# A six-stage fp32 network: two MLP norms and the third layer divide by the norm behind their products

## The reference

```python
def rmsnorm(x, g):
    xf = x.astype(jnp.float32)
    y = xf * lax.rsqrt(jnp.mean(xf * xf, axis=-1, keepdims=True) + EPS)
    return (y * g.astype(jnp.float32)).astype(x.dtype)

# stick_breaking_attention, for a block of 128 queries
z = jnp.einsum('bhqd,bhkd->bhqk', q_blk, kt).astype(jnp.float32) * scale
mask = kpos[None, :] < qpos[:, None]
log_keep = jnp.where(mask, jax.nn.log_sigmoid(-z), 0.0)
log_survive = lax.cumsum(log_keep, axis=3, reverse=True) - log_keep
weights = jnp.where(mask, jnp.exp(jax.nn.log_sigmoid(z) + log_survive), 0.0)

# the odd layer, and the MLP behind each layer
hn = rmsnorm(x, odd_norm[i])
q, k, v = jnp.split(hn @ odd_w_in[i], 3, axis=-1)
x = x + stick_breaking_attention(q, k, v) @ odd_w_out[i]
hn = rmsnorm(x, ffn_norm[layer])
x = x + (jax.nn.silu(hn @ ffn_w_gate[layer]) * (hn @ ffn_w_up[layer])) @ ffn_w_down[layer]
```

## Time and profile before

| | |
|---|---|
| runs | 1703.34, 1696.55, 1700.85 us, median 1700.85 |
| profiled execution | 1705.26 us, its span 1703.5 us |
| PE busy | 1597.6 us (94%) |
| DVE, ACT, POOL busy | 62%, 49%, 23% of the span |
| first MLP from norm to norm | 142.36 to 337.40 us |
| odd layer | 337.40 to 484.08 us |
| second MLP | 484.08 to 679.40 us |

### The profile page before, as it was taken

How to read it: one execution, slowest core, us unless ns; L and a number is a source line. 1 busy time by engine, 2 the same in 40 slices (tenths; PEclk the granted TensorE clock), 3 DMA queues, 4 the chain that set the end, 5 groups by cost and what they waited for, 6 DMA issues and landing times.

```text
span 1703.5 us, 32938 instructions
## 1 busy us (share of the span) xinstructions
PE 1597.6 (94%) x11807; PEld 1448.6 (85%) x11807; DVE 1053.7 (62%) x1973; ACT 832.7 (49%) x1228; POOL 393.4 (23%) x176
## 2 busy tenths in 40 slices
PE   7779999999799999896899989999999999999999
PEld 6668999898589999895689989999999777778887
DVE  7775555512235555717469993067887899985555
ACT  6456444458644444543355655544444444445453
POOL 2001000156330001562267898810000000000000
PEclk9879999999999999898899999999999999999999
DMA  5114555543255555342144545555545445555554
GB/s 215 63 57 134 184 186 186 179 137 100 75 199 185 185 185 181 124 131 72 62 149 164 177 154 166 184 167 164 169 160 166 156 168 167 169 163 195 195 188 159
DMA packets 72557, 264.88 MB, mean 155 GB/s; under 512 B 8080, under 2 KB 8336, under 8 KB 72112
## 3 DMA queue, kind: packets, MB, share of 16 engines
q1 hardware_dynamic: 71744, 261.20, 46.7%
q10 hardware_dynamic: 752, 2.83, 0.5%
HBM read 262.95 MB, written 1.05 MB: 155 GB/s over the span
## 4 chain that ended last, share of the span: by engine, by line
PE 82%; DVE 5%; POOL 5%; issue 4%; ACT 4%; DMA 0%; POOLq 0%; DVEq 0%; ACTq 0%
PE ps L495 25%; PE ps L497 24%; PE ps L496 24%; POOL w_lo L2109 5%; DVE arena L1441 2%; PE ps L972 2%; PE ps L552 1%; PE ps L808 1%; ACT xn L1074 0%; PE ps L588 0%; PE ps L652 0%; DVE w_lo L1441 0%; DVE x_s L1441 0%; ACT w_hi L1047 0%; ACT arena L1191 0%
## 5 line engine op out<-in xcount | busy, mean ns | idle before, releaser
L1047 ACT ACTIVATE w_hi<-ring 128x1024 fp32r<-128x1024 f32 x489 | 516.6, 1057 | 380.1 <-PE ps L497 371.4
L495 PE MATMUL ps<-hT_hi,w_hi 128*128 128x256 f32 x2216 | 639.5, 289 | 18.9 <-POOL w_lo L2109 11.5
L496 PE MATMUL ps<-hT_hi,w_lo 128*128 128x256 f32 x2216 | 628.9, 284 | 0.0
L497 PE MATMUL ps<-hT_lo,w_hi 128*128 128x256 f32 x2216 | 628.8, 284 | 0.0
L2109 POOL TENSOR_TENSOR w_lo<-ring,w_hi 128x1024 fp32r<-128x1024 f32 x151 | 378.8, 2519 | 679.4 <-ACT w_hi L1047 679.0
L1441 DVE TENSOR_TENSOR w_lo<-ring,w_hi 128x1024 fp32r<-128x1024 f32 x338 | 412.6, 1222 | 178.9 <-ACT w_hi L1047 178.5
L495 PEld LDWEIGHTS ps<-hT_hi,w_hi 128*128 128x128 f32 x2216 | 426.9, 193 | 26.1 <-ACT arena L1386 8.7
L496 PEld LDWEIGHTS ps<-hT_hi,w_lo 128*128 128x128 f32 x2216 | 427.2, 193 | 1.6
L497 PEld LDWEIGHTS ps<-hT_lo,w_hi 128*128 128x128 f32 x2216 | 426.7, 193 | 0.0
L495 PE MATMUL ps<-w_hi,a_hi 128*128 128x512 f32 x688 | 275.5, 400 | 3.4 <-DVE a_lo L1441 3.4
L497 PE MATMUL ps<-w_lo,a_hi 128*128 128x512 f32 x688 | 269.4, 392 | 0.0
(11 more groups left out here) (237 smaller groups left out, 1351.1 us busy)
## 6 DMA issues: line engine op xcount, KB each, us to landing
ring<-in_strips SPq DMA_DIRECT2D x489, 512.0 KB, 3.5
const<-in_const SPq DMA_DIRECT2D x1, 1544.0 KB, 12.2
x_s<-in_x SPq DMA_DIRECT2D x2, 512.0 KB, 4.6
arena<-in_rel ACTq DMA_DIRECT2D x1, 1024.0 KB, 6.0
arena<-in_keys ACTq DMA_DIRECT2D x1, 1024.0 KB, 6.4
out<-x_s SPq DMA_DIRECT2D x4, 256.0 KB, 2.1
arena<-in_ssm_bc SPq DMA_DIRECT2D x1, 512.0 KB, 6.8
arena<-in_ssm_b SPq DMA_DIRECT2D x1, 512.0 KB, 8.0
```

The costliest lines, as they stand in the source:

```text
L495: pe.matmul(out, l_hi, r_hi, start=start, stop=False, **kw)
L496: pe.matmul(out, l_lo, r_hi, start=False, stop=False, **kw)
L497: return pe.matmul(out, l_hi, r_lo, start=False, stop=stop, **kw)
L1047: sc.activation(w_hi[:, n % RING, :], ring[:, n % RING, :], ACT.Copy).then_inc(high_ready, 1)
```

## The change

1. In the three norms x is turned raw, by a PE transpose that waits for the residual sums (`raw_norm`). ACT's copies (`parts`) come between its two squares, DVE's ahead of the reciprocals. The diagonal of scales is spread to a row over all partitions by two fp32 products with ones (`widen_scale`) behind the first strips, and DVE copies it out (`take_scale`).
2. In the MLPs DVE multiplies the gate product by the row ahead of ACT's silu, and the up product in `combine`.
3. In the odd layer DVE scales q and k out of PSUM (`project`), ACT scales v per token. The softplus is masked on DVE (a product with 0 and 1) and split in two fp32r halves, and `cum` is two fp32r products for one in fp32. PE runs `z(j)` ahead of `cum(j-1)`; ACT runs `softplus(j)` ahead of `weights(j-1)`; the copies of `ov` move to DVE.
4. The end of the odd layer is written anew: the last pair's scores use banks 4 and 5, so that out strips 0 and 1 run ahead of its sums, and DVE makes the low halves of the out strips, not POOL.

```diff
+            def raw_norm(i):
+                for a in range(NT):
+                    for c in range(KC):
+                        if c % 4 == 0:
+                            pe.wait_ge(x_ready, 4 * (i - 1) + 2 * a + c // 4 + 1)
+                        at = (c % 2) * T + a * P
+                        mm = pe.transpose(ps[:, norm_bank(i, c // 2), at:at + P], x_s[:, a, c * P:(c + 1) * P],
+                                          ident)
+                        if a == NT - 1 and c % 2:
+                            mm.then_inc(turned, 1)
+            def widen_scale(i):
+                pe.wait_ge(diag_ready, NT * (i + 1))
+                for a in range(NT):
+                    mm = pe.matmul(ps[:, 0, a * P:(a + 1) * P], ones, scale_diag[:, a, :], start=True, stop=True)
+                mm.then_inc(scale_wide, 1)
...
                 gate_up(base, 4, fresh=STAGE_OF[name])
+                widen_scale(STAGE_OF[name])
...
-                    pe.wait_ge(sp_masked, j + 1)
+                    pe.wait_ge(sp_low, j + 1)
                     for h in (2 * j, 2 * j + 1):
-                        pe.matmul(ps[:, h % 4, 0:3 * P], k("neg_tri"), o_sp[:, h % 4, :], start=False,
-                                  stop=False, skip_group_check=True)
+                        b = z_bank(h)
+                        for part in (o_sp_hi, o_sp_lo):
+                            pe.matmul(ps[:, b, 0:3 * P], o_tri[:, :], part[:, h % 2, :], start=False, stop=False,
+                                      skip_group_check=True)
...
-                pe.wait_ge(w_masked, 8)
+                pe.wait_ge(w_masked, 7)
                 out_rows(1, "odd", range(2))
+                ov(6)
+                cum(7)
+                out_rows(1, "odd", range(2, 4))
                 ov(7)
-                out_rows(1, "odd", range(2, KC))
+                out_rows(1, "odd", range(4, KC))
...
+                def gate(strip, c, i=None):
+                    ve.wait_ge(strip_done, strip + 1 if i is None else UNROLL * i + (strip + 1))
+                    tt(f_silu[:, c % 2, :], ps[:, 4 + c % 2, 0:T], scale_row, ALU.mult).then_inc(gate_scaled, 1)
...
+                    tt(f_act[:, c % 2, :], ps[:, 6 + c % 2, 0:T], scale_row, ALU.mult).then_inc(up_scaled, 1)
...
+                take_scale(STAGE_OF[name])
+                gate(base, 0)
                 combine(base + 1, 0)
                 low(base + 3)
                 with ve.Fori(0, (FC - 2) // 2) as i:
                     for u in range(2):
                         at = base + 2 + 3 * u
+                        gate(at, 1 + u, i)
                         low(at + 2, i)
                         low(at + 3, i)
                         combine(at + 1, 1 + u, i)
                         low(at + 4, i)
...
+                    ve.wait_ge(sp_ready, j + 1)
+                    ch.link(tt(diagonal(sp), diagonal(sp),
+                               diagonal(bc(o_before, 1, [P, 2, 3 * P])), ALU.mult))
+                    ve.tensor_copy(o_sp_hi, sp).then_inc(sp_high, 1)
+                    ve.wait_ge(sp_high, j + 1)
+                    tt(o_sp_lo, sp, o_sp_hi.bitcast(F32),
+                       ALU.subtract).then_inc(sp_low, 1)
...
             po.wait_ge(low_ready, AT[("odd", "v", 0)])
             lows(("odd", "v", 0), ("odd", "v", 7))
...
+            lows(("odd", "q", 0), ("odd", "k", 1))
+            po.wait_ge(sp_low, 1)
+            lows(("odd", "q", 2), ("odd", "k", 7))
+            po.wait_ge(low_ready, AT[("mlp1", "gate", 0)])
```

More of the change, by code:

```diff
@@ L1068, in norm, with parts @@
                     high_to(first + 1)
+                def parts():
+                    for c in range(KC // 2):
+                        sc.wait_ge(turned, 4 * i + c + 1)
+                        for cc in range(2):
+                            ins = sc.activation(hT_hi[:, 2 * c + cc, :],
+                                                ps[:, norm_bank(i, c), cc * T:(cc + 1) * T], ACT.Copy,
+                                                scale=prm(NORMS[i], 2 * c + cc, 2 * c + cc + 1))
+                        ins.then_inc(hT_high, 1)
                 for a in range(NT):
+                    if i in SCALED_OUT and a == NT - 1:
+                        parts()
                     if i:
@@ L1092, in norm @@
                     sc.activation(e_p[:, 10, :], e_p[:, 7, :], ACT.Sin).then_inc(prm_act, 1)
-                for c in range(KC // 2):
-                    sc.wait_ge(turned, 4 * i + c + 1)
-                    for cc in range(2):
-                        ins = sc.activation(hT_hi[:, 2 * c + cc, :], ps[:, norm_bank(i, c), cc * T:(cc + 1) * T],
-                                            ACT.Copy, scale=prm(NORMS[i], 2 * c + cc, 2 * c + cc + 1))
-                    ins.then_inc(hT_high, 1)
+                if i not in SCALED_OUT:
+                    parts()
                 high_to(first + RING - 1)
@@ L1256, in odd @@
                 for g in range(4):
-                    out_of_pair(("odd", "v"), g, o_v)
+                    high_to(AT[("odd", "v", 2 * g + 1)] + RING - 1)
+                    sc.wait_ge(strip_done, AT[("odd", "v", 2 * g + 1)] + 1)
+                    if g == 0:
+                        sc.wait_ge(diag_ready, 2 * NT + NT)
+                    for a in range(NT):
+                        ins = sc.activation(o_v[:, a, g * T:(g + 1) * T],
+                                            ps[:, 4 + nproj[0] % 2, a * T:(a + 1) * T], ACT.Copy,
+                                            scale=stat[:, 4 + a:5 + a])
+                    ins.then_inc(evac, 1)
+                    nproj[0] += 1
                 def softplus(j):
@@ L1837, in mlp @@
                 at = base + 2 + 3 * (FC - 2)
+                gate(at, FC - 1)
                 low(at + 2)
```

177 lines of the change are left out of this document (121 added, 56 removed).

## The result

| | before | after |
|---|---|---|
| runs, median | 1700.27 us (4 runs, 1696.55 to 1703.34) | 1675.23 us (4 runs, 1673.99 to 1680.97) |
| profiled execution | 1705.26, span 1703.5 | 1675.24, span 1673.3 |
| mean granted clock | 0.970 | 0.977 |

The ratio is 0.986, 95% interval 0.9834 to 0.9885: 1.4% faster. The forecast was 1678, range 1668 to 1690.

What follows compares the result with a forecast made beforehand. PE bounds the MLPs, so gains come at seams and the third layer's heads and end: -13.9 + 1.7 + 2.4 + 0 - 0.8 - 12.4 = -23.0. From 1705.26 that gives 1682.3, on the median 1678, range 1668 to 1690.

Steps and rivals of the forecast that it cites:

- Seams, -13.9: Three norm seams: turning x raw no longer waits for the scale, saving 4.36, 4.79 and 4.71 us, 13.9 in all.
- rival (2): Seams: PE's half clock after a wait may move from the turning onto the first strips, +5 us, 1683; chance 0.2.
- Row of scales and stall, +1.7 and +2.4: Spreading the scales three times costs 1.7 us; a late up-strip low half stalls PE 1.2 us at both MLPs, 2.4.
- Chunks of the MLPs at 0: DVE's two added operations of 0.42 us in each of 44 MLP chunks were priced at 0, hidden beside PE.
- at least 0.5 us of cover: MLP chunks: everything DVE delivers is ready at least 0.5 us before PE's strips need it.
- Heads, -0.8: Third layer's heads: five round trips of 9.1 us and two of 10.4, 66.4 for 67.16; bounds -3 to +4.
- PE waiting some 0.3: Third layer's heads: expected sign that scores come every 9.1 us with PE waiting some 0.3 for DVE's k.
- the second again finds the wrong table, 10.4: Heads: ACT's new order makes the second pair's trip also include a 1.3 us table load, 10.4 us for 9.1.
- End of the layer, -12.4: Third layer, last scores to next norm: PE's work 27.1 plus waits 2.45, 29.55 us for 41.95; bounds -14.9 to -6.4.
- (1) The port of DVE and POOL: Heads: DVE operations held up to 2.2 us by POOL's splits in six pairs, +13 us, 1691; chance 0.12.
- (3): Third layer's end worth half, DVE's one queue being later than counted: -6 for -12.4, 1684; chance 0.13.
- (4): MLP chunks: down strips' low halves and their slots' next loads come late; at 0.8 us per chunk +35, 1713; chance 0.03.

Runs made afterwards that it cites:

- MLP-only kernel: Against the kernel before, only the norms of both MLPs divide behind the products, third layer as before: 1694.0 us for 1698.86, ratio 0.9964.
- the filler's run: Changed kernel plus 11 idle 128-column products on PE in its wait ahead of the second pair's scores: 1674.23 us, ratio 0.9843.
- The fp32 kernel: Changed kernel with the sums over later keys in one fp32 product again, without the halves: 1676.8 us, ratio to before 0.9863.
- The two experiments: Changed kernel with the third layer's end as before: 1686.83 us; with only the out strips' low halves back on POOL: 1677.69 us.
- the second (1696.92 to 1675.57): The changed kernel measured once more, unedited, in one group with three others: 1675.57 us for 1696.92, ratio 0.9879.

## Why the prediction was right

**Seams, -13.9: right.** Square to first product is 3.26 us at all three (143.40 to 146.66, 335.70 to 338.96, 463.44 to 466.69), for 7.63, 8.07 and 7.98. Only the transposes were off: 16 in 2.20 us for 1.9, hidden beside the square. The MLP-only kernel shows the gain of two of the seams by itself. Part of the gain is the clock: rival (2) saw that the old turning ran partly at half clock, but gave no price for an old seam where it did not, and that one was 1.6 us shorter.

**Row of scales and stall, +1.7 and +2.4: right, slightly high.** The MLPs lost 1.63 us each against 1.75, the value part of the third layer 0.48 (29.98 for 29.50) against 0.55. A wait of 1.01 stands where 1.2 was forecast, for the low half that I named; moving the row forward removed it in the first MLP and left 0.23 in the second, which shows that DVE's order and not the load made it late.

**Chunks of the MLPs at 0: right**, by the 0.73 us above. What I called at least 0.5 us of cover was not tried by taking the cover away.

**Heads, -0.8: the sum near, by luck: two of its parts are off, with opposite signs.** (Its terms add up to 66.3, not 66.4, so -0.9.) Measured -1.3: the five later pairs gave 1.2 us more than forecast, the first two 0.7 less. Later pairs take 8.86 us for 9.1: scores to ACT's read 0.98, from there to DVE 3.89, DVE's five rows 3.93 (404.21 to 408.14), and 0.06 to the next scores. DVE's prices were right to 0.01 but for the scaling of q and k, 0.75 us in its row for 0.84; the larger error was the 0.25 us for semaphores, of which 0.06 stand there. PE is busy in 8.82 of 8.86, so the trip and PE's work are nearly equal, and "PE waiting some 0.3" did not show. The first two pairs were forecast at 10.4 each; from scores to scores they take 10.13 and 11.41. The step that failed is "the second again finds the wrong table, 10.4": the trip of that pair is indeed about 10.1, as the filler's run shows, but PE stood 3.26 us ahead of it, fell to half clock and itself became the bound at 11.41. The fp32 kernel shows what the sum had hidden: the halves shorten a pair's work on PE (the pace goes from 9.35 to 8.86) and lengthen the trip, which binds the first pairs. With the table's load moved away the halves are worth 1.1 us.

**End of the layer, -12.4: right, -13.3.** 28.66 for 29.55. The last sums came at S+9.8 (444.58) as forecast, out strip 0 at S+3.33 after 1.05 us of waiting. The two later waits, forecast at 0.45 and 0.6 us, did not come: DVE had out 3's low half at S+13.2, not S+14.25, and out 4's at S+17.1, not S+18.5. PE's 27.61 us of other time stand against 27.1. The two experiments divide a gain of 13.9 us into 10.0 for PE's free work between and 3.9 for DVE in POOL's place. The 13.3 hold for the one trace of before at hand: the other has the old end at 44.56 us, 2.6 longer by its clock.

**Rivals.** (1) The port of DVE and POOL: no DVE operation in the heads of 2 us or more; excluded in the heads for this order. It does come at the end of the layer when POOL makes the low halves of the out strips: operations of 0.29 and 0.42 us took 1.20 and 2.46. The change, which takes that work off POOL, avoids it; the prediction had not counted this as a gain. (2) The clock: 1.00 in the first strips behind the turning at all three seams, so it did not fall there; it fell in the heads instead, and there it cost 1.3 us (11.41 for 10.1). (3) and (4): the end is worth all of its price and more; DVE's wait for ring loads never reached PE in the chunks.

**The whole.** -23.0 forecast; stages -24.7. On medians -25.0 in the first comparison and -21.4 in the second (1696.92 to 1675.57), ratios 0.986 and 0.9879, whose intervals overlap. Setting the sum against the profiled 1705.26, and then taking 4.4 off for the median, was sound: that execution's extra lay in the mixer stage.

## What to carry to other kernels

When a scale per token divides out behind a product, price the pipeline break at the norm (here 4.4 to 4.8 us each) against a stall at the first use of the scale; put the spreading of the scale where its inputs become ready, not where it is handy. Where a stage is bound by a round trip at its start and by TensorE later, an edit that trades one for the other can be worth nothing until the start is mended: look at the first turns of a loop apart from the steady ones. Put independent products into a wait before making the awaited operation faster: that was 10.0 of 13.9 us. And when work moves between DVE and POOL, look in the trace for small operations of DVE beside POOL's splits that take a multiple of their own time, and not only at the mover's pace.

## What the runs showed of the hardware

The same stretch of the same kernel ran at another granted clock from one execution to the next. The mixer stage took 170.8 to 172.3 us in seven traces, 173.3 and 173.5 in two, 175.7 and 176.0 in two and 177.6 in three, among kernels that share its code; 5.0 of the 5.4 us between the two traces of before are PE's busy time at the lower clock, and what makes the clock fall more often there in some executions stays open. In the third layer of the kernel before, the same wait of 4.67 us was followed by full clock from 454 us on in one trace, 3 us after the product that ended the wait, and by half clock until past 462 us in the other, over 8 us after it (products of 512 columns took 0.39 and 0.63 us). The old seam's turning ran at 0.69 in six of seven cases and at 1.00 in the seventh. So a stage that has many short waits carries an uncertainty of some us in a single trace, while a stage that PE fills does not: the sixteen MLPs of nine traces that have the changed kernel's order, without the long issue, took 192.28 to 192.31 us. Idle products in a wait kept the clock at 1.00 where it had fallen in all five traces without them. A row at 0.50 is the level of 1.2 GHz, one at 1.00 that of 2.4.

A load's issue from ACT's queue took 2.18 and 2.20 us in two traces and 0.46 in the other ten with the new seams. It stands ahead of a weight strip's split, and the second MLP took 1.05 us more in both (193.35 and 193.36).

With POOL splitting a strip beside it, a cast of 256 columns on DVE took 1.20 us for 0.29 and three subtractions 2.46, 2.62 and 2.40 for 0.42, and one of POOL's splits 3.14 for 2.4. In the heads, where POOL's splits and DVE's operations fell apart in time, none of DVE's took over 0.96.
